# Two transformer-like layers on one core: delta-rule outputs a round later, norms row by row behind the products, the last norm in row groups

## The reference, cut to what matters

```python
# layer 1
h = rms_norm(x, norm_mix);  proj = h @ w_in
q, k, v = silu(short_conv(...));  gated delta rule, forward and backward, 8 heads of 64:
  v_new = u_i - w_i @ S;  o_i = q_i @ S + a_i @ v_new;  S = S * gl + k_i.T @ v_new
mix = concat(rms_norm(o_f + o_b) * silu(z), spatial_gating(su, sv))
x = x + mix @ w_out
x = x + square(relu(rms_norm(x, norm_ffn) @ w_ff1)) @ w_ff2        # FF = 4096
x = rms_norm(x, norm_final)
# layer 2
merged = sigmoid(gate_a) * (s5 state space branch) + sigmoid(gate_b) * (conv branch)
x = layer_norm(ALPHA * x + merged @ w_o, ln1_g, ln1_b)
hid = silu(x @ w_gate) * (x @ w_up)                                # 2816 hidden
x = layer_norm(ALPHA * x + hid @ w_down, ln2_g, ln2_b)
```

## Time and profile before

| what | us |
|---|---|
| median of 3 runs | 3080.97 |
| the profiled execution's own time | 3082.7 |
| its span | 3080.9 |
| TensorE busy in the span | 2860.5 (93%) |
| mean granted TensorE clock, share of full speed | 0.961 |
| VectorE, ScalarE, GpSimd busy | 1274.8, 722.6, 206.4 |

### The profile page before, as it was taken

The page is one execution under the profiler, slowest core; times in us unless marked ns, Lnnn a source line. Parts: engine busy times, 40 slices in busy tenths (PEclk is TensorE's granted clock), DMA queues, the critical chain, the costliest instruction groups (busy, mean ns, idle before and its releaser), DMA issues.

```text
span 3080.9 us, 33354 instructions
## 1 busy us (share of the span) xinstructions
PE 2860.5 (93%) x13930; PEld 2129.9 (69%) x13930; DVE 1274.8 (41%) x1753; ACT 722.6 (23%) x1168; POOL 206.4 (7%) x120
## 2 busy tenths in 40 slices
PE   5999997885989999999988999999988999999995
PEld 2445557774458888888878888854447888888884
DVE  1474876655043333333347543413125333334334
ACT  4234354221021121211131222220042111121214
POOL 0000324220000000000001111100000000000000
PEclk9999998895999999999999999999988999999998
DMA  4002013203011111111121222262101111112101
GB/s 144 28 28 82 28 68 102 79 29 116 0 55 41 54 45 50 54 41 44 52 80 59 73 73 73 73 258 90 41 14 49 47 54 41 41 41 68 49 19 55
DMA packets 159603, 187.93 MB, mean 61 GB/s; under 512 B 13457, under 2 KB 115089, under 8 KB 158865
## 3 DMA queue, kind: packets, MB, share of 16 engines
q1 hardware_dynamic: 159504, 186.54, 18.6%
HBM read 160.10 MB, written 25.23 MB: 60 GB/s over the span
## 4 chain that ended last, share of the span: by engine, by line
PE 84%; DVE 11%; ACT 3%; issue 2%; DMA 1%; DVEq 0%; SPq 0%; ACTq 0%
PE ps L1112 56%; PE ps L1269 8%; PE ps L841 5%; PE ps L894 4%; DVE sb L1973 2%; PE ps L906 2%; DVE sb L1975 2%; PE ps L813 1%; PE ps L1013 1%; DVE sb L2049 1%; PE ps L1053 1%; PE ps L984 1%; PE ps L1038 1%; PE ps L1049 1%; PE ps L1027 1%
## 5 line engine op out<-in xcount | busy, mean ns | idle before, releaser
L1112 PE MATMUL ps<-H_hi,v_hi 128*128 128x512 f32 x704 | 275.2, 391 | 3.0 <-DVE H_lo L2146 3.0
L1112 PE MATMUL ps<-H_lo,v_hi 128*128 128x512 f32 x704 | 275.0, 391 | 0.0
L1112 PE MATMUL ps<-H_hi,v_lo 128*128 128x512 f32 x704 | 274.9, 390 | 0.0
L1269 PE MATMUL ps<-sb 128*128 128x512 f32 x576 | 249.6, 596 | 6.4 <-ACT sb L1645 2.9
L1269 PEld LDWEIGHTS ps<-sb 128*128 128x128 f32 x576 | 109.8, 191 | 145.7 <-issue 143.3
L1112 PE MATMUL ps<-H_hi,w_hi 128*128 128x512 f32 x512 | 200.0, 391 | 5.5 <-DVE w_lo L2151 5.5
L1112 PE MATMUL ps<-H_lo,w_hi 128*128 128x512 f32 x512 | 199.9, 390 | 0.0
L1112 PE MATMUL ps<-H_hi,w_lo 128*128 128x512 f32 x512 | 199.8, 390 | 0.0
L1112 PE MATMUL ps<-w_hi,ff_hi 128*128 128x512 f32 x512 | 199.2, 389 | 0.0
L1112 PE MATMUL ps<-w_lo,ff_hi 128*128 128x512 f32 x512 | 199.2, 389 | 0.0
L1112 PE MATMUL ps<-w_hi,ff_lo 128*128 128x512 f32 x512 | 199.2, 389 | 0.0
(11 more groups left out here) (289 smaller groups left out, 4802.0 us busy)
## 6 DMA issues: line engine op xcount, KB each, us to landing
wraw<-in_w_ff SPq DMA_DIRECT2D x32, 1024.0 KB, 5.2
traw<-in_w_in SPq DMA_DIRECT2D x28, 512.0 KB, 4.3
sb<-in_w_in SPq DMA_DIRECT2D x6, 2048.0 KB, 8.1
vraw<-in_w_gate SPq DMA_DIRECT2D x22, 512.0 KB, 4.1
vraw<-in_w_up SPq DMA_DIRECT2D x22, 512.0 KB, 5.4
vraw<-in_w_down SPq DMA_DIRECT2D x11, 1024.0 KB, 4.9
sb<-in_x SPq DMA_DIRECT2D x4, 2048.0 KB, 9.8
sb<-c_rows SPq DMA_DIRECT2D x16, 512.0 KB, 4.7
```

Source lines behind the costliest of these rows:

```text
L1112: mm = nc.tensor.matmul(out_ap, stationary(a, k), moving(c, k), start=(k == 0 and n == 0), stop=(k == kts - 1 and n == 2))
L1269: mm = nc.tensor.matmul(ps[:, b, :], lhs, rhs, start=(n == 0), stop=(n == len(terms) - 1))
```

## The change

Three groups of edits. In the delta rule, the outputs of round i-1 are made in four parts inside round i, behind the state products and between the first solve steps; all scores move behind them; decayed queries get a third buffer; `row_decay` moves behind the first solve step. In both norms ahead of a feed-forward, each row tile is normed and turned while PE goes on with the second half's products, two rows behind; the last two rows are turned after two tiles of the first feed-forward round, which is therefore written out and no part of the loop. The order of tiles in the first product of `ff_round` is changed so that both tiles of the first half of the rows come first. The last norm is done in groups of 3, 3 and 2 rows, and POOL adds the shift of rows 0 to 5.

```diff
+
+        def behind(*parts):
+            return [("o", i - 1, p) for p in parts] if i > 0 else []
+        order += [("kS", i, d) for d in both] + behind(0, 1)
+        order += pair("y", 0) + behind(2) + pair("w", 1) + behind(3)
+        order += pair("y", 1) + ahead("kk", 0) + pair("w", 2) + ahead("kq", 0)
+        order += pair("y", 2) + ahead("kk", 1) + pair("w", 3) + ahead("kq", 1)
+        order += pair("y", 3)
...
         if more:
             order += [("kv", i, d) for d in both]
-        order += [("o", i, d) for d in both]
+    order += [("o", NT - 1, p) for p in range(4)]
...
+    order = [("w", t, 0) for t in range(NT)]
+    for t in range(NT):
+        order += [("w", t, 1)] + [("t", t - 2, h) for h in range(2) if t > 1]
+    order += [("t", t, h) for t in (NT - 2, NT - 1) for h in range(2)]
...
-               for at_q in (AT_W + 7168, AT_CONST + MASKS * P + 2 * D + 32)]
+               for at_q in (AT_W + 7168, AT_CONST + MASKS * P + 2 * D + 32, AT_CONST + 2 * P)]
...
-            wait_drained(sp, G_WOUT, 15)
             ff_load(0, 0)
+            wait_full(sp, *mixed("t", NT - 1, 1))
             ff_load(1, 0)
...
             for h in range(2):
+                if h == 1:
+                    wait_full(sp, G_MRG, 31)
...
-                sp.wait_ge(ln_rows, 8 + j + 1)
+                if j < 6:
+                    sp.wait_ge(ln_rows, 8 + j + 1)
+                else:
+                    sp.wait_ge(ln_last, j - 5)
...
-                        mm = nc.tensor.matmul(ps[:, b, cols], ATm[i % 2][d][:, h, :], yv[i % 2][d][:, cols],
-                                              start=False, stop=(h % 2 == 1))
-                mm.then_inc(full[b], 1)
+            def outputs(i, *parts):
+
+                for p in parts if i >= 0 else ():
+                    d = p // 2
...
+                outputs(i - 1, 0, 1)
+                solve(i, 0)
+                outputs(i - 1, 2)
+                for d in both:
+                    forward(i, d, 1)
+                outputs(i - 1, 3)
+                solve(i, 1)
                 if more:
                     scores("kk", i + 1, 0)
-                solve(i, 0)
+                for d in both:
+                    forward(i, d, 2)
+                if more:
+                    scores("kq", i + 1, 0)
+                solve(i, 2)
                 if more:
                     scores("kk", i + 1, 1)
                 for d in both:
-                    forward(i, d, 1)
-                solve(i, 1)
-                if more:
-                    scores("kq", i + 1, 0)
-                for d in both:
-                    forward(i, d, 2)
-                solve(i, 2)
+                    forward(i, d, 3)
                 if more:
                     scores("kq", i + 1, 1)
-                for d in both:
-                    forward(i, d, 3)
                 solve(i, 3)
                 if more:
                     for d in both:
                         update(i, d)
-                for d in both:
-                    outputs(i, d)
+            outputs(NT - 1, 0, 1, 2, 3)
 
             for t in range(NT):
...
+            for t in range(NT):
+                mixed_rows(t, 0)
+            pe.wait_ge(slab_in[1], 16 * 4)
+            for t in range(NT):
+                mixed_rows(t, 1)
+                if t > 1:
+                    pe.wait_ge(norm_rows, NT + t - 1)
+                    turn_row(mixed, xn3[(t - 2) % 3], t - 2)
+            norm_base[0] += NT
+            rows_ready(mixed, range(4))
+
             def split_product(out_ap, stationary, moving, kts):
...
+                for k0 in range(8):
+                    ft, h = 2 * (k0 // 4) + k0 % 2, k0 // 2 % 2
+                    if k0 % 4 == 0:
+                        pe.wait_ge(w_lo, i * 4 + k0 // 4 + 1)
+                    if k0 == 2 and isinstance(i, int) and i == 0:
+                        for j in (NT - 2, NT - 1):
+                            pe.wait_ge(norm_rows, NT + j + 1)
+                            turn_row(mixed, xn3[j % 3], j)
+                        rows_ready(mixed, range(4, NT))
...
+                    product(*merged("w", t, h), [(M[:, k, t * P:(t + 1) * P], wo_half[h][:, k, :]) for k in range(KT)])
+                    if h == 1 and t > 1:
+                        pe.wait_ge(ln_rows, t - 1)
+                        turn_row(merged, X[:, t - 2, :], t - 2)
+            rows_ready(merged, range(4))
...
                     nc.scalar.copy(yv[i % 2][0][rows, :], ps[rows, b, :]).then_inc(drained[b], 1)
+                    if s == 0 and i + 1 < NT:
+                        row_decay(i + 1)
                 if i + 2 < NT:
                     decay(i + 2)
-                    row_decay(i + 2)
 
             root(NT * HEADS)
...
+            for t in range(NT):
+                for h in range(2):
+                    wait_drained(act, *mixed("w", t, h))
+                nc.scalar.activation(xn3[t % 3], X[:, t, :], ACT.Square, accum_out=ssum[:, t:t + 1]).then_inc(norm_sums, 1)
+                root(1, t)
+                if t > 1:
+                    round_row(mixed, t - 2, Fs[0])
+                if t == 5:
+                    round_slab(0, 0)
...
+            for t in range(NT):
+                for h in range(2):
+                    wait_drained(act, *merged("w", t, h))
+                row_sum(t, 0)
+                if t > 0:
+                    root(1, t - 1)
+                    row_scaled(t - 1, t)
+                row_squares(t, 0)
+                if t > 1:
+                    round_row(merged, t - 2, Hs[0])
+            root(1, NT - 1)
+            row_scaled(NT - 1, NT)
...
+            last_sum(0)
+            last_sum(1)
+            last_squares(0)
+            last_sum(2)
+            last_squares(1)
+            last_sum(3)
+            last_squares(2)
+            last_sum(4)
+            last_squares(3)
+            root(3, 0)
+            last_sum(5)
+            last_squares(4)
+            last_scaled(1, 0, 1, 2)
+            last_sum(6)
+            last_squares(5)
+            last_sum(7)
+            last_squares(6)
+            root(3, 3)
+            last_squares(7)
+            last_scaled(2, 3)
+            root(2, 6)
+            last_scaled(2, 4, 5)
+            last_scaled(3, 6, 7)
...
             for i in range(NT):
                 if i + 1 < NT:
                     decayed_queries(i + 1)
+                    clear(i + 1)
                 if i + 2 < NT:
                     decay_args(i + 2)
                 if i + 1 < NT - 1:
                     decayed_keys(i + 1)
-                if i + 2 < NT:
...
 
+            pool.wait_ge(gain_in, 16 * 7)
+            for j in range(6):
+                pool.wait_ge(ln_gained, NT + j + 1)
+                G.tensor_tensor(X[:, j, :], X[:, j, :], shift, ALU.add).then_inc(ln_rows, 1)
...
+                collect(i - 1, 0, 1)
+                second_drain(i, 0)
+                collect(i - 1, 2)
                 if more:
-                    state_decay(i)
-                ahead("kk", 0)
-                second_drain(i, 0)
-                ahead("kk", 1)
+                    state_decay(i, 0)
                 less_forward(i, 0, 1)
                 less_forward(i, 1, 1)
+                collect(i - 1, 3)
+                if more:
+                    state_decay(i, 1)
                 second_drain(i, 1)
-                ahead("kq", 0)
+                ahead("kk", 0)
                 less_forward(i, 0, 2)
                 less_forward(i, 1, 2)
+                ahead("kq", 0)
                 second_drain(i, 2)
-                ahead("kq", 1)
+                ahead("kk", 1)
                 less_forward(i, 0, 3)
                 less_forward(i, 1, 3)
+                ahead("kq", 1)
                 second_drain(i, 3)
                 if more:
                     state_add(i)
-                collect(i)
-
-
-            for d in both:
-                ready("o", NT - 1, d)
+            collect(NT - 1, 0, 1, 2, 3)
...
+            for t in range(NT):
+                mixed_drain(t, 1)
+                if t > 0:
+                    scale_row(t - 1)
+                dve.wait_ge(norm_sums, NT + t + 1)
+                V.tensor_scalar(rs_arg[:, t:t + 1], ssum[:, t:t + 1], 1.0 / D, EPS, ALU.mult, ALU.add).then_inc(root_ask, 1)
+                if t > 1:
+                    rest_row(mixed, t - 2, Fs[0], Fs[1], 0)
+                if t == 5:
+                    rest_slab(0, 0)
+            scale_row(NT - 1)
             def ff_round(i, last):
...
+            for t in range(NT):
+                merged_drain(t, 1)
+                if t > 0:
+                    row_arg(t - 1, 1, 0)
+                    row_root(t - 1, 1)
+                row_mean(t, 0)
+                if t > 0:
+                    first_norm(t - 1)
+                if t > 1:
+                    rest_row(merged, t - 2, Hs[0], Hs[1], 2)
+            row_arg(NT - 1, 1, 0)
+            row_root(NT - 1, 1)
+            first_norm(NT - 1)
 
...
```

(56 more changed lines are left out.)

363 lines of the change are left out of this document (190 added, 173 removed).

## The result

The changed kernel takes 2987.01 us (median of 4 executions, 2986.0 to 2991.45) against 3080.76 (4 executions, 3080.04 to 3082.13): a ratio of 0.9698, 95% interval 0.9681 to 0.9715. It is 93.8 us faster; the forecast was 79.8 and 3001 us, and the measured time lies 0.01 us inside the lower end of the range. Executions of one kernel lie up to 7 us apart here, so where two kernels differ by less than 10 us I give the lowest of five beside the median, or the length of the stage in the traces.

The account below looks back on a forecast made before the run. TensorE work nearly throughout, so gains only where it stands still or runs at 1.2 GHz, in four places: 45.4 + 11.9 + 23.5 - 1 = 79.8 us off 3082.7, 3002.9; median 3001 us, range 2987 to 3022 (forecast's own 2993 to 3010).

Parts of the forecast that it names:

- Part 1: Delta-rule recurrence: rounds shrink from 31.9 to 25.4 us over seven intervals, 45 us won; bounds 33 and 51.
- allowance of 0.8 us a round: Recurrence: added to the derived 24.6 us round for added waits, late collects and clock, giving 25.4.
- Part 2: Norm behind the output products: hides under products except turning (14.0 us) and a 1.3 us wait; 12 us won, bounds 8 to 14.
- Part 3: Norm behind the merge products: row chain of 8.45 us just hides under TensorE's 8.62; 23.5 us won, bounds 13.5 to 26.
- Part 4: Last norm: POOL and VectorE exclude each other, so splitting the work loses 1 us, between -8 and +2.
- the recurrence gained more than the forecast and not less: Rival, recurrence smaller: delayed solution copies or remaining half-clock stretches leave 33 us instead of 45; 3013 us, chance 0.13.
- the merge chain: Rival, merge norm: its chain takes 10 us a row, longer than TensorE's row; 3011 us, chance 0.09.
- POOL and VectorE did not run side by side: Rival, last norm: both engines run beside each other, ending 8 us before 3077.84; 2992 us, chance 0.11.
- new tile order: Rival, feed-forward rounds: slab 1 rounded later delays each of 8 rounds; slower, 3081 us or more, chance 0.02.
- what would show it: Signs: carried states about 25.4 us apart, merge rows 8.6, one 1 to 3 us wait per stream, last write 28 to 30 after TensorE.

Follow-up runs that it names:

- undivided run: Changed kernel with all four output parts of the round before directly behind the carried state, none in later gaps: 3003.85 us, ratio 0.9745.
- first experiment: Kernel before with only the recurrence's new order; norms, feed-forward and end as before: 3024.59 us, ratio 0.9815.
- second measurement: The changed kernel, unaltered, measured again beside later experiments: 2986.01 us (5 executions), ratio 0.9695.

## Why the prediction was right, and where it was wrong

**What bounds the kernel** was read rightly: nearly all of the gain lies in the places named, and the streams run without a gap at the price per product that they had (687.31 / 3024 = 0.227 us). The forecast of 79.8 us was 14.0 short of the measured 93.8; by the two spans it is 16.8 short, of which 11.4 are part 1.

**Part 1** was forecast at 45.4 us and brought 50.8 + 6.0 = 56.8. The derived round of 24.6 us is what the trace shows, 24.63. Two things were mis-sized. The allowance of 0.8 us a round for late collects and lost clock was not needed: the granted clock went from 0.91 to 1.00 in the rounds, with TensorE busy 140.1 of 147.8 us instead of 154.7 of 191.3. (In the undivided run it is 1.00 as well, with 139.1 of 158.2 us.) That is 7 x 0.8 = 5.6 us. And the last round was not in the sum at all: I counted seven intervals between rounds and took the eighth for unchanged, where it ran at 1.2 GHz before and runs at 2.4 for most of its length now, 6.0 us. 45.4 + 5.6 + 6.0 = 57.0. The first experiment shows 57.6 for this part alone, and the undivided outputs show the two effects apart.

**Part 2** was forecast at 11.9 and brought 14.8. The turning was mis-sized: the sum has 16 blocks a row, but a row of 1024 is eight, and the earlier trace rows show 64 blocks for eight rows. So TensorE pays 8 x 0.87 = 7.0 and not 14.0. On the other side the wait behind the second tile is 3.38 instead of 1.3, and 1.7 us more go in the stretch at 1.2 GHz behind it (a granted clock of 0.66 over the 5.1 us from 840.92), for which I had nothing: 25.2 + 2 - 7.0 - 3.4 - 1.7 = 15.1, and 0.3 stay unplaced.

**Part 3** was forecast at 23.5 and brought 23.1, by errors that cancel. The turning is 7 us cheaper here too. But TensorE's row is then 7.74 and not 8.62, and my chain of 8.45 (seen: 8.15) no longer hides: rows come late by 1.70 and twice 0.41 us. The last row costs 1.36 + 3.47 instead of 2.5, and the clock behind it about 2. 40.7 - 7.0 - 2.5 - 4.8 - 2 = 24.4; 1.3 us of the difference to 23.1 I can't place. The long wait I had sized for one row: the last two rows are turned together, so four roundings (2.04 us) and four rests (2.48) stand between the turning and the stream. In the merge norm ScalarE has the first tile's SILU with a table load of 1.28 us between the two rows, which looks like the cause; but the output norm has no table load there and waits 3.38 us all the same. What the table load adds was not tested. The run with the rows one behind removed the whole wait.

**Part 4** was forecast at a loss of 1 us, and 0.2 was seen. The reason holds: the two engines exclude each other, and the run without POOL's shifts is 4.4 us faster in this stage.

**The rivals.** None came true: the recurrence gained more than the forecast and not less, the merge chain held TensorE up by 2.5 us in all and not 10, POOL and VectorE did not run side by side in operations with two inputs. The feed-forward rounds' new tile order cost nothing. As to what would show it, the carried states came 24.6 and not 25.4 us apart, merge rows 7.74 to 8.15 and not 8.6, and the wait behind the turned rows was longer than the 1 to 3 us that I gave it.

That the time lies in the range is luck: it held by 0.01 us, and the second measurement lies 1 us below it. The two larger errors, the last round and the turning, lay on the side of more gain, and the range's lower end had been drawn from the bounds of single parts and not from both at once.

## What to carry to other kernels

Cost every round of a loop, the last one too, and cost it with the clock that the new order will have: work that fills gaps is worth more than its own length where the gaps had brought TensorE down to 1.2 GHz. Count the instructions of a moved step once more against the row that gives their duration, and when a term gets smaller look again at what it was hiding. Before a share of VectorE's two-operand work goes to POOL, look in the trace for a two-input VectorE operation beside one of POOL; if the one that began second, however short, ends only when the first has ended, keep the work on VectorE and look for an operation less.

## What was not expected of the hardware

- The granted clock falls without a long pause: in the last round of the changed kernel TensorE is busy 7.04 us of the 11 up to 664 us, with no wait above 1 us, and the clock is 0.50 behind it; two thrown-away products in each of five gaps of at most 1 us kept it at 2.4 GHz and were worth 4.8 us of this stage. The Trainium skill, "TensorE: Matmul & The Clock Gate", section "What's actually happening", lists the lower clock as the state of an idle engine, set by how busy the engine has been; this trace shows it behind an engine that was busy most of the time.
- Two executions of one kernel differ by 3 us or more because the granted clock is lower for some us in a stage that no edit touched: 210.3 us at 1.00 and 213.6 at 0.98 for the same products. A gain of a few us is read from its own stage.
- A turned 128x128 block takes 0.109 us and one record, a product of the same shape two records and 0.28 us.
- POOL holds even the smallest two-operand step of VectorE until it is done itself: 0.16 us became 2.32. A one-operand step begun 0.59 us into a POOL shift took 0.15.
